# A two-layer decoder step on one core: linear layers end by column halves, square sums go to TensorE, residual additions to VectorE

## The reference

```python
def rmsnorm(x, g):
    y = x * lax.rsqrt(jnp.mean(x * x, axis=-1, keepdims=True) + RMS_EPS)
    return y * g

# each layer, three times: x = x + rmsnorm(f(rmsnorm(x, g_pre)), g_post)
#   f = token mixer (pooling and sparse attention, or a recurrent block)
#   f = cross attention with 256 memory tokens, output projection w_xo
#   f = swiglu: (silu(h @ w_gate) * (h @ w_up)) @ w_down
```

## Time and profile before

| | |
|---|---|
| median of 3 runs | 2060.88 us (2060.76 to 2062.21) |
| the profiled execution | 2063.55 us, span 2061.5 us |
| busy share: TensorE, its weight loads | 90%, 81% |
| busy share: VectorE, ScalarE, GpSimd | 49%, 34%, 12% |
| granted TensorE clock, mean | 0.947 |
| DMA | 124 GB/s mean |

### The profile page before, as it was taken

How to read it: one execution, slowest core, us unless ns; L and a number is a source line. 1 busy time by engine, 2 the same in 40 slices (tenths; PEclk the granted TensorE clock), 3 DMA queues, 4 the chain that set the end, 5 groups by cost and what they waited for, 6 DMA issues and landing times.

```text
span 2061.5 us, 31823 instructions
## 1 busy us (share of the span) xinstructions
PE 1845.8 (90%) x13423; PEld 1672.8 (81%) x13423; DVE 1001.9 (49%) x1405; ACT 694.6 (34%) x1155; POOL 254.8 (12%) x231
## 2 busy tenths in 40 slices
PE   5997997668897989999999899898979799999995
PEld 3786675448886679999999889897957699999994
DVE  6894784334563346444422394837432654444123
ACT  2113453344342433222222235644224432222221
POOL 2330001222120021000000012022110300000001
PEclk9997898889999989999999989999999899999997
DMA  5895003763364212222222212244451122222221
GB/s 219 333 366 204 1 1 143 286 245 134 103 214 189 77 62 72 89 84 92 81 86 94 82 62 80 87 164 153 155 223 42 58 86 82 92 82 89 85 94 52
DMA packets 59655, 254.73 MB, mean 124 GB/s; under 512 B 10224, under 2 KB 10624, under 8 KB 45904
## 3 DMA queue, kind: packets, MB, share of 16 engines
q1 hardware_dynamic: 40320, 135.39, 19.9%
q0 software_dynamic: 14656, 109.53, 13.6%
q10 hardware_dynamic: 4576, 8.34, 1.1%
HBM read 244.89 MB, written 12.68 MB: 125 GB/s over the span
## 4 chain that ended last, share of the span: by engine, by line
PE 77%; DVE 12%; DMA 5%; ACT 4%; issue 1%; POOL 0%; SPq 0%; ACTq 0%; POOLq 0%; DVEq 0%
PE ps L1592 73%; DVE work L1111 3%; PE ps L1843 2%; DVE big L1172 1%; PE ps L1760 1%; DVE work_r L1133 1%; DVE rinv L1095 1%; DVE wring_r L1125 1%; ACT whi L683 1%; DMA mc<-in_slck,idx 1%; DVE x L1114 1%; DMA mc<-in_memv 1%; DMA mc<-in_memk 1%; DMA big<-in_slck,idx 1%; ACT work L856 1%
## 5 line engine op out<-in xcount | busy, mean ns | idle before, releaser
L1592 PE MATMUL ps<-work_r,whi 128*128 128x272 f32 x4352 | 762.7, 293 | 47.8 <-ACT work_r L695 27.5
L1592 PEld LDWEIGHTS ps<-work_r,whi 128*128 128x128 f32 x4352 | 633.7, 191 | 62.0 <-issue 40.9
L1592 PE MATMUL ps<-work_r,wring_r 128*128 128x272 f32 x2432 | 512.8, 293 | 0.0
L683 ACT ACTIVATE whi<-wring 128x1024 fp32r<-128x1024 f32 (+1 forms) x232 | 242.3, 1045 | 791.8 <-PE ps L1592 789.4
L1125 DVE TENSOR_TENSOR wring_r<-wring,whi 128x1024 fp32r<-128x1024 f32 (+1 forms) x232 | 283.4, 1224 | 438.0 <-ACT whi L683 437.9
L1592 PEld LDWEIGHTS ps<-work_r,wring_r 128*128 128x128 f32 x2432 | 388.9, 193 | 0.0
L1592 PE MATMUL ps<-mc_r,whi 128*128 128x272 f32 x1216 | 242.8, 289 | 0.0
L1592 PE MATMUL ps<-big_r,whi 128*128 128x272 f32 (+1 forms) x960 | 198.3, 294 | 13.9 <-DVE wring_r L1125 13.9
L1592 PEld LDWEIGHTS ps<-mc_r,whi 128*128 128x128 f32 x1216 | 188.9, 190 | 0.0
L1592 PEld LDWEIGHTS ps<-big_r,whi 128*128 128x128 f32 x960 | 155.5, 196 | 15.2 <-DVE wring_r L1125 15.1
L1592 PE MATMUL ps<-mc_r,wring_r 128*128 128x272 f32 x704 | 145.9, 289 | 0.0
(11 more groups left out here) (296 smaller groups left out, 2022.3 us busy)
## 6 DMA issues: line engine op xcount, KB each, us to landing
wring<-w_ffn SPq DMA_DIRECT2D x88, 512.0 KB, 3.5
mc<-in_memk POOLq DMA_DIRECT2D x16, 1024.0 KB, 8.0
mc<-in_memv POOLq DMA_DIRECT2D x16, 1024.0 KB, 7.9
wring<-w_down SPq DMA_DIRECT2D x32, 512.0 KB, 3.5
wring<-w_w_out SPq DMA_DIRECT2D x16, 512.0 KB, 4.1
wring<-w_mk SPq DMA_DIRECT2D x16, 512.0 KB, 3.4
wring<-w_mv SPq DMA_DIRECT2D x16, 512.0 KB, 4.0
wring<-w_xq SPq DMA_DIRECT2D x16, 512.0 KB, 4.1
```

What stands on the lines that cost most here:

```text
L683: act.activation(dst, src, ACT.Copy).then_inc(S("w_hi"), 1)
L1592: return pe.matmul(out, lhsT, rhs, start=start, stop=stop, **kw)
```

## The change

Four norms (`pxat0`, `pffn0`, `pxat1`, `pffn1`) are made by halves of 272 columns. For the last weight block before such a norm TensorE does all of half 0, then half 1, and the stats lie between: `ssum` and half 0 of the last square in the middle of half 1, half 1 of the square behind it. ScalarE squares and takes the root by halves and no longer copies chunk 7 to `y`; VectorE takes the reciprocal by halves and scales chunk 7 from the accumulator. The weight copy that stood ahead of the last eviction comes behind the second root, and its low part goes between chunks of the residual (`tail`), after the multiplication of chunk 5.

Three pre-norms (`ffn_0`, `mix1`, `ffn_1`) get their square sums on TensorE, one chunk at a time, in the `m=0` phase of the next linear layer, right behind the matmuls of the next chunk; ScalarE alternates scaled copy and square. GpSimd's and VectorE's part of these sums goes away, and the pre-norm's accumulator comes ahead of block 0's instead of behind two blocks.

All residual additions, also those of `pmix`, are VectorE's, one behind each multiplication, and GpSimd's `add` is gone. Some semaphores are merged or renamed.

```diff
+HALVED = ["pxat0", "pffn0", "pxat1", "pffn1"]
+BY_CHUNK = ["ffn_0", "mix1", "ffn_1"]
...
+def stats_at(name):
+
+    return 0 if INNER[name] in BY_CHUNK else AFTER
...
-            def add(r):
-
-                for c in range(0, 8, 2):
-                    pool.wait_ge(S("y_scaled"), 8 * r + c + 1)
-                    pool.tensor_tensor(x[:, c, :], x[:, c, :], y[:, c, :], ALU.add).then_inc(S("x_ready0"), 1)
...
-                    act.wait_ge(S("sq_summed"), 6 * n + max(c - 2, 1))
+                    act.wait_ge(S("sq_summed"), 6 * n + (c - 1 if name in BY_CHUNK else max(c - 2, 1)))
...
+            def ahead_squared(name):
+
+                for c in range(8):
+                    ahead(name, [c])
+                    square(name, c, x[:, c, :])
...
+                if not halved:
+                    root(norm)
+                    return
...
+                square_half(norm, g, 0)
+                root_half(norm, 0)
+                square_half(norm, g, 1)
+                root_half(norm, 1)
+                if last + 2 < NBLK:
+                    w_hi(last + 2)
...
-                ahead(f"ffn_{l}")
+                ahead_squared(f"ffn_{l}")
...
+                if name in HALVED:
+                    for a_ in range(2):
+                        dve.wait_ge(S("rms_ready"), RMS0[name] + a_ + 1)
+                        dve.reciprocal(halves(rinv[:, :])[:, a_, :], halves(rms[:, :])[:, a_, :]).then_inc(S("rinv_ready"), 1)
...
                 for c in range(9):
-                    if c < 8:
+                    if c == 7 and source:
+                        g = acc_of(source, 7)
+                        acc_done(dve, g)
+                        dve.scalar_tensor_tensor(out=halves(y[:, c, :]), in0=accp[g % 4],
...
+                    elif c < 8:
                         dve.tensor_tensor(y[:, c, :], y[:, c, :], rinv[:, :], ALU.mult).then_inc(S("y_scaled"), 1)
-                    if c and c % 2 == 0:
+                    if c:
                         dve.wait_ge(S("y_scaled"), 8 * r + c)
-                        dve.tensor_tensor(x[:, c - 1, :], x[:, c - 1, :], y[:, c - 1, :], ALU.add).then_inc(S("x_ready1"), 1)
+                        dve.tensor_tensor(x[:, c - 1, :], x[:, c - 1, :], y[:, c - 1, :], ALU.add).then_inc(S("x_ready"), 1)
                     if between and c in (0, 3, 6, 8):
                         w_next(between, 3 + (0, 3, 6, 8).index(c))
+                    if tail is not None and c == 5:
+                        w_lo(tail)
...
+                half(0, range(tiles)).then_inc(S("half_done"), 1)
+                half(1, range(tiles // 2))
+                acc_free(pe, gs)
+                pe.wait_ge(S("sq_summed"), 6 * (NORM[norm] + 1))
+                for a_ in range(2):
+                    mm(accp[gs % 4][:, a_, :], C("ones"), halves(ssum[:, :])[:, a_, :], True, False)
+                pe.wait_ge(S("sq_ready"), SQ0[norm] + 8)
+                mm(accp[gs % 4][:, 0, :], C("ones"), halves(sq[:, 1, :])[:, 0, :], False, True).then_inc(S("half_stats"), 1)
+                half(1, range(tiles // 2, tiles)).then_inc(ready[g % 4], 1)
+                pe.wait_ge(S("sq_ready"), SQ0[norm] + 9)
+                mm(accp[gs % 4][:, 1, :], C("ones"), halves(sq[:, 1, :])[:, 1, :], False, True).then_inc(ready[gs % 4], 1)
+
+            def chunk_stats(norm, c):
+
+                gs = ACC["s_" + norm]
+                if not c:
+                    acc_free(pe, gs)
+                pe.wait_ge(S("sq_ready"), SQ0[norm] + c + 1)
+                for a_ in range(2):
+                    last = mm(accp[gs % 4][:, a_, :], C("ones"), halves(sq[:, c % 2, :])[:, a_, :], c == 0, c == 7)
+                if c < 6:
+                    last.then_inc(S("sq_summed"), 1)
...
+                            if by_chunk and not m and c:
+                                chunk_stats(by_chunk, c - 1)
+                        if by_chunk and not m:
+                            chunk_stats(by_chunk, 7)
```

More of the change, by code:

```diff
@@ L133, in acc_of @@
 def acc_of(name, i):
-    return ACC[name] + i + (name in INNER and i >= AFTER)
+    return ACC[name] + i + (name in INNER and i >= stats_at(name))
 PER = {"mv": 4, "down": DB}
@@ L706, in evict_y @@
                 down = name.startswith("down")
-                for m in range(8):
+                halved = norm in HALVED
+                for m in range(7 if halved else 8):
                     g = acc_of(name, m)
@@ L974, in layer_end @@
                 evict_y(f"xo{l}", f"pxat{l}", 6 * l + 3)
-                ahead(f"ffn_{l}")
+                ahead_squared(f"ffn_{l}")
                 name = f"ffn{l}"
[L977 to L980, removed]
+                root(f"ffn_{l}")
                 def hid_parts(gs, m, hid, hh, k, i=0):
@@ L992, in hid_parts @@
                         act.activation(hh[j], hid[j], ACT.Copy).then_inc(S("hid_hi"), 1)
-                for m in range(1, AFTER):
+                for m in range(AFTER):
                     w_next(name, m)
-                root(f"ffn_{l}")
                 hid_parts([acc_of(name, j) for j in range(4)], 0, [big[:, j, :] for j in range(2)],
@@ L1004, in _ @@
             layer_end(0)
-            ahead("mix1")
-            for m in range(8):
-                square("mix1", m, x[:, m, :])
-                if m == 5:
-                    w_next("w_in1a", 0)
-            for m in range(1, AFTER):
-                w_next("w_in1a", m)
+            ahead_squared("mix1")
             root("mix1")
-            for m in range(AFTER, 6):
+            for m in range(6):
                 w_next("w_in1a", m)
@@ L1061, in _ @@
             for c in range(0, 8, 2):
-                for q in range(2):
-                    act.wait_ge(S(f"x_ready{q}"), 20 + c // 2 + 1)
+                act.wait_ge(S("x_ready"), 40 + c + 2)
                 act.dma_start(o["yp"][:, c:c + 2, :], x[:, c:c + 2, 0:TP]).then_inc(S("out_y"), 16)
@@ L1199, in _ @@
                                            sample(big[rows, Q + c, TP:T]))
-            last.then_inc(S("qbd_ready"), 1)
+            last.then_inc(S("prep_dve"), 1)
             acc_done(dve, ACC["cmp", 7])
@@ L1213, in _ @@
                 last = dve.tensor_scalar(mv4[:, q, 32 * q:32 * q + 31], s32[:, 1, 0:31], 1.0 / 32, None, ALU.mult)
-            last.then_inc(S("means_ready"), 1)
+            last.then_inc(S("prep_dve"), 1)
             dve.wait_ge(S("out_pool"), 16)
@@ L1217, in _ @@
             dve.memset(spn, 0.0)
-            dve.memset(pce, 0.0).then_inc(S("zeroed"), 1)
+            dve.memset(pce, 0.0).then_inc(S("prep_dve"), 1)
             for hb in range(2):
@@ L1484, in layer_end @@
                            [hidhi[:, 2 * i + (2 + j), :] for j in range(2)], FC * l + 2, i)
-                for m in range(8 * DB):
+                for m in range(8 * DB - 1):
                     b = WSEG[f"down{l}"][0] + m + 2
@@ L1492, in layer_end @@
                     dve.memset(cext[:, :, 0:3], 0.0).then_inc(S("conv_zero"), 1)
-                residual(f"pffn{l}", 3 * l + 2)
+                residual(f"pffn{l}", 3 * l + 2, None, f"down{l}", None if l else WSEG["down0"][0] + 8 * DB + 1)
             layer_end(0)
-            sums("mix1")
-            for m in range(AFTER):
-                w_next("w_in1a", m)
+            w_next("w_in1a", 0)
             inverse("mix1")
+            w_next("w_in1a", 1)
             dve.wait_ge(S("conv_past"), 16)
@@ L1660, in linear @@
                         last.then_inc(ready[g % 4], 1)
-                    if name in INNER:
+                    if name in INNER and not by_chunk:
                         stats(INNER[name])
@@ L1787, in _ @@
             pe.wait_ge(S("pa_out"), 4)
-            pe.wait_ge(S("qbd_ready"), 1)
+            pe.wait_ge(S("prep_dve"), 1)
             opened = set()
```

114 lines of the change are left out of this document (80 added, 34 removed).

## The result

The changed kernel takes 2036.08 us (median of 4 runs, 2031.82 to 2040.55), the kernel before beside it 2060.82 us. The ratio is 0.9877 with an interval of 0.9861 to 0.9894: 24.7 us less, by the interval between 22 and 29. The forecast was 18.8 us less, 2042, in a range of 2033 to 2052. The result lies in the range; it is faster than the likeliest case and 2 us from rival (b).

What follows compares the result with a forecast made beforehand. TensorE bounds the kernel, so only gaps between matmuls can be won: 9.3 us in three inner passages (after xo0, down0, xo1), 4.1 at the end, 5.4 in pmix, sum 18.8 off 2060.9, giving 2042; range 2033 to 2052.

Steps and rivals of the forecast that it cites:

- rival (b): Clock returns 3.4 us after restart and the pmix gap stays warm: 26.6 us won, 2034; chance 0.12.
- Until rinv: After xo and down of both layers, norm by halves: rinv 5.2 us after zero instead of 8.2.
- zero: Time 754.55 in the xo0 to ffn0 stretch, where the last weight block is issued and the stats begin.
- No table load between squares and roots: ScalarE alternates Square and Sqrt without extra table loads; otherwise 2.6 us by four, time near 2052.
- The chunk phase: TensorE from restart at 8.1 to phase end 22.8, then m=2 at 31.25; 3.15 us won after xo0.
- C: Time TensorE spends at the lower clock after the restart, taken as 5.9 us; each us does 0.45 us of work.
- The loop: ScalarE square, stats, next square: bounds the chunks about evenly with TensorE, 1.4 us a chunk at full clock.
- rival (a): Clock returns as late as before, after 10.6 us: 0.6 us won after xo0, down0, xo1 each; 2049.5, chance 0.2.
- The end: After the last down: x7 at 15.5 where it took 19.6; output transfers unchanged; 4.1 us won.
- pmix: In each layer's mk blocks, additions on VectorE shorten the work: 2.7 us each, 5.4 in all, bounds 1 and 4.5 each.
- Rival (c): Stats phase at the lower clock end to end: m=2 at 41.7, 7.3 later; 2073, chance 0.04.
- Rival (d): Gains after xo0, down0, xo1 given back behind them by caches' transfers or the recurrence: 2054 to 2058, chance 0.1.

## Why the prediction was right, and where it wasn't

**Until rinv: right.** Forecast 5.2 us after zero, measured 5.23 (750.59); square of a half 0.40 (0.4 forecast), root 0.49 (0.49), reciprocal 1.85 (1.85). The old `rinv` was complete at 8.19, not 8.22, by the rows. The restart came at 8.15 (8.1). With the norm whole the passages lose all they had won, so without this part the others win nothing there.

**No table load between squares and roots: right.** A load stands only ahead of the first half root of a passage. The price that the Trainium skill (ScalarE: Activation LUTs, Table sets) sets on alternating functions of different sets was not paid: square and root alternated here without one.

**The chunk phase: right in sum by small errors of opposite sign.** `C` was 3.8, 4.3 and 5.3 us in the three passages, not 5.9 (in the `xo0` passage 753.5 to 757.3). The phase took 13.9, 14.0 and 14.35 us from the restart to `m=1`, where the forecast has 14.7. The loop, named in the forecast as "about evenly" with TensorE's own 1.4 us, went at 1.54; with the measured `C` the forecast's sum gives 13.6, 13.8 and 14.4, so this cost 0.3 us at most. From there to `m=2` it took 9.0 us, not 8.45, since the next weight block was split later than forecast (the wait of 0.63 us for `wring_r` above). So `m=2` stood at 31.05 (forecast 31.25), in the `down0` passage at 31.1 (31.35); by stretches the three won 9.4 us (9.3). Moved alone, the clock gave 1.4 us a passage, the loop 0.5 to 0.9. Two readings were off without harm: the lower clock of the kernel before lasted to 777.2, 10.95 us instead of 10.6, which makes rival (a) 0.4 us a passage; and the mean of 1.1 us for an `x_lo` holds the waits beside GpSimd, alone it is 0.78.

**What the sums by chunk are for: missing.** In the forecast they bought an earlier `m=2` with more work for TensorE. That a GpSimd sum can be kept waiting by VectorE's low parts, 4.8 us for 1.4, and that the longer wait ahead of the stats can bring the clock down, wasn't seen, though the earlier trace rows had multiplications of 1.86 us beside GpSimd. It did not touch the sum, since the change has both edits; it made my expectations for two of the parts wrong.

**The end: right up to the last addition, wrong behind it.** 4.1 us forecast, 4.08 measured (19.59 to 14.13 from the last matmul, whose own stretch is 1.4 longer). The step that failed is "Output transfers behind it are the same". They were, but the program had not been waiting for them: 4.0 us more, by GpSimd's drain. It was to be found in the trace of before, in SyncE's wait of 4.1 us behind the outputs, which I hadn't read.

**pmix: the step right, the bound taken too low.** Work of VectorE 2.70 (2.7), with the clock 4.0, inside the bounds of 1 and 4.5. 8.1 us for 5.4.

So 18.8 + 4.0 (drain) + 2.7 (clock in `pmix`) + 0.1 = 25.6 us by stretches, where the medians differ by 24.7 with 2 to 3 us of uncertainty. Rival (b) at 2034 came near with the warm `pmix` and a `C` that is almost right for some passages, but took 4.5 us a passage; those with a `C` of 3.8 won 3.35 and 3.4. That its time is nearer than the forecast's is in part luck, since it has no term for the 4.0 us of the drain. Rival (a) fell with `C`. Rival (c), the stretch at 1.2 GHz from end to end, fell too; in the kernel with the filled gap, waits of 0.91 and 0.44 us between groups left the clock at 1.00. What the Trainium skill (TensorE: Matmul & The Clock Gate, A second HAM failure mode) says of small waits between groups of matmuls didn't happen there. Rival (d) fell: the stretches behind the passages are unchanged (`ffn0`, from `m=2` on, 252.75 and 252.64).

Open is where the last 3 us of the 16 come from that the run with the norm whole lost; its interval allows the 12.9 of the stretches. Open is also what decides whether GpSimd's first sum gets in between VectorE's low parts: not tried was the same block with the first square moved by some hundredths of a microsecond.

## What to carry to other kernels

An operation that moves from GpSimd to a busy VectorE is judged with what stays on GpSimd: look in the trace whether that still gets in between VectorE's two-input instructions, and what a longer wait of TensorE behind it does to the clock. Read the end of a program to its last record: if GpSimd's last instruction lies less than its drain ahead of the last output, an instruction of a tenth of a microsecond costs several. In a gap of TensorE that ends in dense work, time one term for the clock, one for each loop through another engine and one for the next weight block; here each was off by less than 1 us, some one way and some the other. Two executions of one kernel show how far the clock's term varies.

## What the runs showed of the hardware

GpSimd's closing drain ends 8.7 us after its last instruction, after a 1.74 us addition as after a 0.10 us memset. A GpSimd sum beside eight back-to-back VectorE instructions with two SBUF inputs took 4.82 us instead of 1.4 in six passages, ending 1.2 us after the last of them, and 1.35 us in nine others, where VectorE's took 1.88 us instead of 0.78. After an idle time of 5.4 us the clock was at 1.2 GHz and came back 3.8 to 5.3 us after a dense restart, in six passages of two executions of one kernel; 4.6 us of matmuls put in that gap kept it at 2.4 GHz, through the waits of 0.9 and 0.4 us that followed. Idle times ahead of eight stats records after dense matmuls brought it down to 1.2 GHz in four passages (2.3 to 3.8 us) and left it at 2.4 GHz in two (1.65 and 3.21 us), so their length alone did not decide. A half of a 544 column operation cost ScalarE 0.40 of 0.62 us and 0.49 of 0.72, VectorE's reciprocal 1.85 of 3.55: two halves cost ScalarE 29 and 36% more than the whole, the reciprocal 4%.
